# Expert gate and up projections as three fp32r products, with the rows stationary and the weights split a block ahead

## The chip, the cores and the metric

The kernel runs on one core of one Trainium2 chip. The metric is the time of one execution on the device in microseconds (us); 3158.83 us is the median of three executions of the kernel before. PE is the matrix engine, DVE the vector engine, ACT the scalar engine, POOL the GpSimd engine, SP the engine that here only issues transfers.

## The reference, cut to what matters

Two transformer blocks run on 1024 rows of 1024 floats. The first ends in a mixture of experts: each row goes to 2 of 32 experts. Rows are sorted by expert into blocks of 128, each block of one expert, and each block computes:

```python
def run_block(args):
    xb, e = args                                             # xb: 128 x 1024
    hid = jax.nn.silu(xb @ w_gate[e]) * (xb @ w_up[e])       # 1024 x 512 each
    return hid @ w_down[e]                                   # 512 x 1024

yb = lax.map(run_block, (buf.reshape(n_blocks, MOE_BLOCK, D), block_e)).reshape(n_rows, D)
y = jnp.zeros((T, D), jnp.float32).at[tok_s].add(yb[dest].astype(jnp.float32) * w_s[:, None])
```

All weights and rows are fp32. In the run profiled the routing makes 32 blocks. The rest of the two layers (a pooling and mLSTM mixer before, windowed, dilated and latent attention after) is not touched.

## The kernel before

`route` leaves, in SBUF, the row numbers of each block (`idx`), the expert of each block (`block_e`) and the number of blocks (`n_blocks`). `experts` then runs a loop over the blocks on every engine, with the block number in a register. Each engine has its own instruction order, written out by hand, and the engines meet at semaphores. `combine` then gathers the two rows of `y_dram` for each token.

A matmul's first operand is stationary (it is loaded into the array), its second moves. `D` is 1024 (`KT` = 8 slices of 128), the expert width 512 (`FT` = 4 slices), `GC` = 4 chunks of two slices. `HALF` is 512, one PSUM bank of fp32. In the profile a matmul's operands are printed moving first, then stationary.

For each block:

- SP loads gate and up in eight chunks of 512 KB, each into the place that PE has finished with (semaphore `used`), then the four chunks of down.
- POOL copies the block's row numbers to `idx` and gathers its 128 rows into `xg` with an indirect transfer.
- PE runs gate and up as plain fp32 products: the stationary operand is a 128 x 128 piece of the weights, the moving one is `xT`, the transposed rows. The result comes out transposed, as 4 slices of hid columns by 128 rows, so hid is already in the form that the down product needs. Then it transposes the next block's rows (`turn`, eight transposes), and runs down.
- Down is computed from fp32r parts. An fp32r operand is rounded to fewer bits. `high` is x rounded, `low` is x minus high, and a product of fp32 accuracy is high x high + high x low + low x high: `multiply_split`, three products.
- ACT makes the high parts of the down weights (L1309), DVE the low parts (`low_part`, L155). ACT computes Silu of gate; DVE multiplies by up and splits hid. Both copy `xT` from PSUM, and both copy half of the result to `y`; ACT issues the store.

The places of the gate and up weights are single: a chunk is loaded again while PE works on the others.

Of the kernel before, what the change touches and what calls it, by code (L numbers as in the profile page):

```python
# [8 lines left out]
ALU = mybir.AluOpType  # L9
ACT = mybir.ActivationFunctionType  # L10
AX = mybir.AxisListType
F32 = mybir.dt.float32
# [3 lines left out]
P = 128  # L16
S = 1024
# [1024 lines left out]
def route(nc, K, R, w_rg, b_rg, w_re, b_re, slot_tok):  # L1042
# [3 lines left out]
    with ExitStack() as ctx:  # L1046
# [27 lines left out]
        with nc.Block() as block:  # L1074
# [55 lines left out]
            def _(dve):  # L1130
# [69 lines left out]
                link(dve.tensor_copy(R["n_blocks"][:, :], pend[0:1, cur, EXPERTS - 1:EXPERTS]))  # L1200


def experts(nc, K, R, h_dram, y_dram, w_gate, w_up, w_down):
# [3 lines left out]
    CH = 2 * GC + FT  # L1207
    with ExitStack() as ctx:
        sc = Scope(nc, ctx, "moe")
        wg = sc.sb("wg", [P, KT, D_EXP])  # L1210
        wu = sc.sb("wu", [P, KT, D_EXP])
        wd = sc.sb("wd", [P, FT, D])
        xg = sc.sb("xg", [P, D])
        xT = sc.sb("xT", [P, KT, P])
        idx = sc.sb("idx", [P, 1], I32)
        sil = sc.sb("sil", [P, HALF])
        hid = sc.sb("hid", [P, FT, P])

        hid_parts = sc.sb("hid_parts", [P, 2, FT, P], F32R)
        wd_parts = sc.sb("wd_parts", [P, 2, FT, D], F32R)  # L1220
        wd_high, wd_split, hid_made = sc.sem("wd_high"), sc.sem("wd_split"), sc.sem("hid_made")
        y = sc.sb("y", [P, D])
        loaded = [sc.sem(f"w{c}") for c in range(CH)]
        used, gathered, idx_ready, xt_made, xt_act, xt_dve, sil_ready, hid_ready, y_act, y_dve, y_stored, settled, settled_act = [sc.sem(n) for n in
            ("used", "gathered", "idx_ready", "xt_made", "xt_act", "xt_dve", "sil_ready", "hid_ready", "y_act", "y_dve", "y_stored", "settled", "settled_act")]
        wg_d = w_gate.rearrange("e (c k p) f -> (e c) p k f", p=P, k=2)
        wu_d = w_up.rearrange("e (c k p) f -> (e c) p k f", p=P, k=2)
        wd_d = w_down.rearrange("e (c p) d -> (e c) p d", p=P)
        nb_ap = R["n_blocks"][0:1, 0:1]
        with nc.Block() as block:  # L1230
            @block.sync
            def _(sp):
                nb = sp.value_load(nb_ap, min_val=1, max_val=BLOCKS)
                with sp.Fori(0, nb) as i:
                    e = sp.value_load(R["block_e"][0:1, bass.ds(i, 1)], min_val=0, max_val=EXPERTS - 1)
                    for c in range(GC):

                        for which, (dst, src) in enumerate(((wg, wg_d), (wu, wu_d))):
                            n = 2 * c + which
                            sp.wait_ge(used, i * CH + n + 1)  # L1240
                            sp.dma_start(dst[:, 2 * c:2 * c + 2, :], src[bass.ds(e * GC + c, 1), :, :, :].rearrange("a p k f -> p (a k) f")).then_inc(loaded[n], 16)
                    for f in range(FT):
                        n = 2 * GC + f
                        sp.wait_ge(wd_split, i * FT + f + 1)
                        sp.dma_start(wd[:, f, :], wd_d[bass.ds(e * FT + f, 1), :, :].rearrange("a p d -> p (a d)")).then_inc(loaded[n], 16)

            @block.gpsimd
            def _(pool):
                nb = pool.value_load(nb_ap, min_val=1, max_val=BLOCKS)
                with pool.Fori(0, nb + 1) as i:  # L1250
                    pool.wait_ge(xt_made, i + 1)
                    pool.tensor_copy(idx[:, :], R["idx"][:, bass.ds(i, 1)]).then_inc(idx_ready, 1)
                    pool.wait_ge(idx_ready, i + 1)
                    pool.sem_inc(settled, 1)
                    pool.indirect_dma_start(out=xg[:, :], out_offset=None, in_=h_dram,
                                            in_offset=bass.IndirectOffsetOnAxis(ap=idx[:, 0:1], axis=0)).then_inc(gathered, 16)
                    pool.wait_ge(gathered, i * 16 + 16)

            def turn(pe):
                for k in range(KT):  # L1260
                    mm = pe.transpose(ps[:, 4 + k // 4, (k % 4) * P:(k % 4 + 1) * P], xg[:, k * P:(k + 1) * P], ident[:, :])
                mm.then_inc(xt_made, 1)

            @block.tensor
            def _(pe):
                pe.sem_inc(used, CH)
                pe.sem_inc(xt_made, 1)
                pe.wait_ge(gathered, 16)
                turn(pe)
                nb = pe.value_load(nb_ap, min_val=1, max_val=BLOCKS)  # L1270
                with pe.Fori(0, nb) as i:
                    pe.wait_ge(xt_act, i + 1)
                    pe.wait_ge(xt_dve, i + 1)
                    for c in range(GC):
                        for which, w in enumerate((wg, wu)):
                            pe.wait_ge(loaded[2 * c + which], i * 16 + 16)
                            for k in (2 * c, 2 * c + 1):
                                for f in range(FT):

                                    mm = pe.matmul(ps[:, which, f * P:(f + 1) * P], w[:, k, f * P:(f + 1) * P], xT[:, k, :],  # L1280
                                                   start=(k == 0 and f == 0), stop=(k == KT - 1), skip_group_check=True)
                            mm.then_inc(used, 1)
                    pe.wait_ge(gathered, i * 16 + 32)
                    turn(pe)
                    pe.wait_ge(y_act, i + 1)
                    pe.wait_ge(y_dve, i + 1)
                    for f in range(FT):
                        pe.wait_ge(wd_split, i * FT + (FT + f + 1))
                        if f % 2 == 0:
                            pe.wait_ge(hid_ready, i * 2 + (f // 2 + 1))  # L1290
                        for n in range(2):
                            cols = slice(n * HALF, (n + 1) * HALF)
                            mm = multiply_split(pe, ps[:, 2 + n, :], (hid_parts[:, 0, f, :], hid_parts[:, 1, f, :]),
                                                (wd_parts[:, 0, f, cols], wd_parts[:, 1, f, cols]), f == 0, f == FT - 1)
                        mm.then_inc(used, 1)

            @block.scalar
            def _(act):
                act.sem_inc(y_act, 1)

                act.dma_start(y_dram[BLOCKS * P:(BLOCKS + 1) * P, 0:P], ident[:, :]).then_inc(y_stored, 16)
                act.wait_ge(xt_made, 2)
                act.activation(xT[:, 0:4, :], ps[:, 4, :].rearrange("p (k t) -> p k t", t=P), ACT.Copy).then_inc(xt_act, 1)
                nb = act.value_load(nb_ap, min_val=1, max_val=BLOCKS)
                with act.Fori(0, nb) as i:
                    act.wait_ge(used, i * CH + CH)
                    for f in range(FT):
                        act.wait_ge(loaded[2 * GC + f], i * 16 + 16)
                        act.activation(wd_parts[:, 0, f, :], wd[:, f, :], ACT.Copy).then_inc(wd_high, 1)  # L1309
                    act.wait_ge(used, i * CH + (CH + 2 * GC - 1))  # L1310
                    act.activation(sil[:, :], ps[:, 0, :], ACT.Silu).then_inc(sil_ready, 1)
                    act.wait_ge(xt_made, i + 3)
                    act.activation(xT[:, 0:4, :], ps[:, 4, :].rearrange("p (k t) -> p k t", t=P), ACT.Copy).then_inc(xt_act, 1)
                    act.wait_ge(used, i * CH + 2 * CH)
                    act.wait_ge(y_stored, i * 16 + 16)
                    act.activation(y[:, 0:HALF], ps[:, 2, :], ACT.Copy).then_inc(y_act, 1)
                    act.wait_ge(y_act, i + 2)
                    act.wait_ge(y_dve, i + 2)
                    act.dma_start(y_dram[bass.ds(i * P, P), :], y[:, :]).then_inc(y_stored, 16)
                act.wait_ge(y_stored, nb * 16 + 16)  # L1320
# [3 lines left out]
            def _(dve):  # L1324
                dve.sem_inc(y_dve, 1)
                dve.sem_inc(wd_split, FT)
                dve.wait_ge(xt_made, 2)
                dve.tensor_copy(xT[:, 4:8, :], ps[:, 5, :].rearrange("p (k t) -> p k t", t=P)).then_inc(xt_dve, 1)  # L1328
                nb = dve.value_load(nb_ap, min_val=1, max_val=BLOCKS)
                with dve.Fori(0, nb) as i:  # L1330
                    for f in range(FT):
                        dve.wait_ge(wd_high, i * FT + (f + 1))
                        low_part(dve, wd_parts[:, 1, f, :], wd[:, f, :], wd_parts[:, 0, f, :]).then_inc(wd_split, 1)
                    dve.wait_ge(sil_ready, i + 1)
                    dve.wait_ge(used, i * CH + (CH + 2 * GC))
                    for q in range(2):
# [1856 lines left out]
```

## Time and profile before

| what | value |
|---|---|
| median of three executions | 3158.83 us (3152.17 to 3163.78) |
| the profiled execution | 3161.66 us |
| its span, first to last instruction | 3159.9 us |
| mean granted TensorE clock | 0.933 of full speed |
| PE busy | 2745.1 us, 87% |
| DVE busy | 1190.5 us, 38% |
| ACT busy | 989.1 us, 31% |
| POOL busy | 374.8 us, 12% |
| bytes moved | 451.17 MB, mean 143 GB/s |

Shares are of the whole span, over stages that have different limits. The expert stage takes about 700 us of it, from about 902 to 1605 us. Busy time of PE counts overlapping matmuls once. Times in the rows are microseconds from the start of the span unless they are marked ns.

### The profile page before, as it was taken

To read this page: it belongs to the slowest core of one execution; us is meant where nothing else is said; L and a number is where in the kernel's file an instruction comes from. 1 tells how busy PE (TensorE), PEld (TensorE's weight loads), DVE (VectorE), ACT (ScalarE), POOL (GpSimd) and SP (SyncE) were. 2 spreads that over 40 slices of the span, in tenths; PEclk is the share of its full clock that TensorE was granted. 3 is DMA by queue.
4 is the path that set the end of the run, shared out by engine and by line. 5 is a ranking of instruction groups with operands and counts; after the bars stand their busy time and mean duration, and the time that the engine had idled before them with its cause. 6 is when DMAs were issued, how large, how long until landed. Compare 5 with 4: busy or idle time off the path is not lost. (4 is left out here: it accounts for less than half of the span.)

```text
span 3159.9 us, 40572 instructions
## 1 busy us (share of the span) xinstructions
PE 2745.1 (87%) x15466; PEld 2277.5 (72%) x15466; DVE 1190.5 (38%) x2498; ACT 989.1 (31%) x1418; POOL 374.8 (12%) x388
## 2 busy tenths in 40 slices
PE   5999799989749999999928999788897988899996
PEld 3887666669749999999926888467797775455586
DVE  4542611122323433334343042366533124555522
ACT  4223311111013343344333153132323235344431
POOL 0000200000020000000021062223120000022120
PEclk9999899999569999999968999899999989999998
DMA  3110281120169999999954294466640312000121
GB/s 91 40 47 14 104 309 40 34 91 23 56 210 345 339 347 345 340 346 347 340 189 130 74 256 131 123 168 143 147 125 1 107 36 47 5 14 15 41 91 61
DMA packets 309981, 451.17 MB, mean 143 GB/s; under 512 B 89612, under 2 KB 183564, under 8 KB 309725
## 3 DMA queue, kind: packets, MB, share of 16 engines
q1 hardware_dynamic: 267664, 326.11, 32.6%
q0 software_dynamic: 26016, 89.15, 8.3%
q10 hardware_dynamic: 16172, 34.17, 3.2%
q8 instruction: 84, 1.38, 0.2%
q14 instruction: 45, 0.36, 0.0%
HBM read 354.88 MB, written 92.19 MB: 141 GB/s over the span
## 5 line engine op out<-in xcount | busy, mean ns | idle before, releaser
L1280 PE MATMUL ps<-moe_xT,moe_wg 128*128 128x128 f32 x2048 | 251.3, 276 | 1.0 <-DVE moe_xT L1328 1.0
L1280 PE MATMUL ps<-moe_xT,moe_wu 128*128 128x128 f32 x2048 | 250.2, 275 | 0.0
L1280 PEld LDWEIGHTS ps<-moe_xT,moe_wg 128*128 128x128 f32 x2048 | 242.9, 193 | 4.0 <-issue 1.4
L1280 PEld LDWEIGHTS ps<-moe_xT,moe_wu 128*128 128x128 f32 x2048 | 239.7, 192 | 0.0
L155 DVE TENSOR_TENSOR moe_wd_parts<-moe_wd,moe_wd_parts 128x1024 fp32r<-128x1024 f32 x128 | 148.5, 1220 | 113.4 <-ACT moe_wd_parts L1309 113.4
L2926 PE MATMUL ps<-lattn_pT,c_v 128*65 128x512 f32 (+3 forms) x384 | 150.6, 487 | 0.0
L2969 ACT ACTIVATE lattn_pT<-ps 128x512 f32<-128x512 f32 (+1 forms) x160 | 92.0, 575 | 186.8 <-PE ps L2912 185.6
L148 PE MATMUL ps<-ab_h,abp_w 128*128 128x512 f32 x336 | 134.1, 399 | 3.5 <-DVE abp_w L155 3.5
L149 PE MATMUL ps<-ab_h,abp_w 128*128 128x512 f32 x336 | 133.5, 397 | 0.0
L150 PE MATMUL ps<-ab_h,abp_w 128*128 128x512 f32 x336 | 133.4, 397 | 0.0
L316 PE MATMUL ps<-ident,n_h 128*128 128x128 f32 x256 | 38.6, 327 | 105.4 <-DVE n_h L290 62.5
L148 PE MATMUL ps<-mix_h,merge_w 128*128 128x512 f32 x256 | 115.2, 450 | 14.8 <-DVE merge_w L155 10.2
L1309 ACT ACTIVATE moe_wd_parts<-moe_wd 128x1024 fp32r<-128x1024 f32 x128 | 125.8, 1048 | 6.8 <-DMA moe_wd<-in_w_e_down_dram 6.4
L2164 PE MATMUL ps<-att_qx,att_kx 65*128 65x256 f32 (+1 forms) x512 | 111.7, 350 | 17.4 <-DVE att_sT L2359 17.4
L148 PE MATMUL ps<-moe_wd_parts,moe_hid_parts 128*128 128x512 f32 x256 | 103.1, 403 | 13.7 <-DVE moe_hid_parts L155 13.7
L316 PEld LDWEIGHTS ps<-ident,n_h 128*128 128x128 f32 x256 | 37.7, 174 | 106.2 <-DVE n_h L290 95.2
L3027 DVE TENSOR_REDUCE lattn_mxr<-ps 128x1 f32<-128x128 f32 (+6 forms) x112 | 77.3, 690 | 91.5 <-PE ps L2892 91.1
L2256 ACT ACTIVATE att_sT<-att_sT 128x512 f32<-128x512 f32 (+1 forms) x104 | 63.1, 613 | 147.8 <-DVE att_sT L2359 143.4
L2164 PEld LDWEIGHTS ps<-att_qx,att_kx 65*128 65x128 f32 x512 | 84.3, 199 | 26.4 <-issue 15.7
L149 PE MATMUL ps<-mix_h,merge_w 128*128 128x512 f32 x256 | 102.7, 401 | 0.0
L150 PE MATMUL ps<-mix_h,merge_w 128*128 128x512 f32 x256 | 102.7, 401 | 0.0
L148 PE MATMUL ps<-mix_h,proj_w 128*128 128x512 f32 x256 | 101.2, 396 | 0.0
(512 smaller groups left out, 6553.4 us busy)
## 6 DMA issues: line engine op xcount, KB each, us to landing
moe_wg<-in_w_e_gate_dram SPq DMA_DIRECT2D x128, 512.0 KB, 4.6
moe_wu<-in_w_e_up_dram SPq DMA_DIRECT2D x128, 512.0 KB, 4.8
moe_wd<-in_w_e_down_dram SPq DMA_DIRECT2D x128, 512.0 KB, 10.2
y_rows<-merge_zero POOLq DMA_DIRECT2D x49, 512.0 KB
y_rows<-moe_y ACTq DMA_DIRECT2D x32, 512.0 KB, 5.5
qk_parts<-abp_high POOLq DMA_DIRECT2D x58, 256.0 KB, 12.3
qk_parts<-abp_full POOLq DMA_DIRECT2D x58, 256.0 KB, 12.2
abp_raw<-in_ab_w_in_dram SPq DMA_DIRECT2D x22, 512.0 KB, 5.2
```

Source lines behind the costliest of these rows:

```text
L148: pe.matmul(out, a[0], b[0], start=start, stop=False)
L149: pe.matmul(out, a[0], b[1], start=False, stop=False)
L150: return pe.matmul(out, a[1], b[0], start=False, stop=stop)
L155: return dve.tensor_tensor(low, x, high.bitcast(F32), ALU.subtract)
L316: mm = pe.transpose(ps[:, u % 8, j * P:(j + 1) * P], h[:, half * 4 + j, k * P:(k + 1) * P], ident[:, :])
L1280: mm = pe.matmul(ps[:, which, f * P:(f + 1) * P], w[:, k, f * P:(f + 1) * P], xT[:, k, :], start=(k == 0 and f == 0), stop=(k == KT - 1), ...
L1309: act.activation(wd_parts[:, 0, f, :], wd[:, f, :], ACT.Copy).then_inc(wd_high, 1)
L2164: mm = pe.matmul(ps[:, 4 + g % 2, off:off + w], block_of(kx[0:HD + 1, s, :], c, r, n), queries, start=True, stop=True, skip_group_check=True)
L2256: act.activation(sT[:, g % SUMS, 0:total], sT[:, g % SUMS, 0:total], ACT.Exp, scale=SC_AB).then_inc(e_done, 1)
L2926: mm = pe.matmul(ps[0:C_V + 1, acc + half, q0 + skip - half * HALF:HALF], v, pT[:, g % SUMS, off + skip:off + n], start=(b == 0), stop=(j ...
L2969: act.activation(pT[:, g % SUMS, 0:total], ps[:, 4 + g % 2, 0:total], ACT.Exp, scale=C_SCALE).then_inc(e_done, 1)
L3027: dve.tensor_reduce(mxr[:, what:what + 1], src[:, 0:w], AX.X, ALU.max)
```

## The change

Gate and up become `multiply_split` products, as down is. Now the transposed rows are stationary (high and low part, `xT[:, 0]` and `xT[:, 1]`) and the weights move, 512 columns at a time. All three weights have a high, a low and a raw place: SP loads into the raw one, ACT writes high, DVE low; for two of the four down chunks POOL computes low (`ON_POOL`). The result of gate and up is now rows by columns, so hid is transposed by four further transposes (`turn_hidden`), and split from PSUM.

The loops are reordered: in iteration j PE runs gate of block j+1, the hid transposes of j, up of j+1, the row transposes of j+2 and down of j. ACT and DVE split gate and up of block j+2 in the same iteration. Block 0 and a part of block 1 stand ahead of the loop, the last two blocks' ends behind it; the loop runs `n_blocks - 2` times, and `n_blocks` becomes three numbers (n, n-1, n-2), with three more DVE operations in `route`.

The contraction index is laid out as `(p c k)` instead of `(c k p)`, so a partition of a chunk is one run of 4 KB of memory instead of two of 2 KB. To match, the row transposes read every eighth column of `xg` (`xg_cols`).

```diff
+        xT = sc.sb("xT", [P, 2, KT, P], F32R)
+        wg_d = w_gate.rearrange("e (p c k) f -> e p c (k f)", c=GC, k=2)
+        xg_cols = xg[:, :].rearrange("t (p k) -> t k p", k=KT)
+        ON_POOL = 2
...
             @block.sync
+                with sp.Fori(0, loops) as j:
+                    e = expert_of(j + 2)
+                    load_gate(j + 2, e)
+                    load_up(j + 2, e)
+                    load_down(j + 1, expert_of(j + 1))
...
             @block.gpsimd
+                def low_down(b):
+                    for i in range(ON_POOL):
+                        f = FT - ON_POOL + i
+                        pool.wait_ge(d_high, b * FT + (f + 1))
+                        pool.tensor_tensor(wd[1][:, f, :], wd[2][:, f, :], wd[0][:, f, :].bitcast(F32), ALU.subtract).then_inc(d_split_pool, 1)
+                with pool.Fori(0, loops) as j:
+                    low_down(j)
+                    gather(j + 3)
...
             @block.tensor
+                def gate_up(b, bank, w, split, used):
+                    for c in range(GC):
+                        pe.wait_ge(split, b * GC + (GC + c + 1))
+                        for k in range(2):
+                            n = 2 * c + k
+                            mm = multiply_split(pe, ps[:, bank, :], (xT[:, 0, n, :], xT[:, 1, n, :]), (w[0][:, c, k, :], w[1][:, c, k, :]), n == 0, n == KT - 1)
+                        mm.then_inc(used, 1)
+                with pe.Fori(0, loops) as j:
+                    gate(j + 1)
+                    turn_hidden(j)
+                    up(j + 1)
+                    turn_x(j + 2)
+                    down(j)
...
             @block.scalar
+                def high(b, w, loaded, used, n, made, c):
+                    act.wait_ge(loaded[c], b * 16 + 16)
+                    act.wait_ge(used, b * n + (c + 1))
+                    act.activation(w[0][:, c], w[2][:, c], ACT.Copy).then_inc(made, 1)
+                def out(b):
+                    act.wait_ge(d_used, b * FT + 2 * FT)
+                    act.wait_ge(y_stored, b * 16 + 16)
+                    act.activation(y[:, 0:HALF], ps[:, 2, :], ACT.Copy).then_inc(y_act, 1)
+                    act.wait_ge(y_act, b + 2)
+                    act.wait_ge(y_dve, b + 2)
+                    act.dma_start(y_dram[bass.ds(b * P, P), :], y[:, :]).then_inc(y_stored, 16)
+                with act.Fori(0, loops) as j:
+                    for f in range(FT - 1):
+                        high(j, wd, d_loaded, d_used, FT, d_high, f)
+                    silu(j + 1)
+                    hidden_high(j)
+                    high(j, wd, d_loaded, d_used, FT, d_high, FT - 1)
+                    for c in range(GC):
+                        high(j + 2, wg, g_loaded, g_used, GC, g_high, c)
+                    rows_high(j + 2)
+                    for c in range(GC):
+                        high(j + 2, wu, u_loaded, u_used, GC, u_high, c)
+                    out(j)
...
             @block.vector
+                with dve.Fori(0, loops) as j:
+                    for f in range(FT - ON_POOL):
+                        low(j, wd, FT, d_high, d_split, f)
+                    hidden_low(j)
+                    for c in range(GC):
+                        low(j + 2, wg, GC, g_high, g_split, c)
+                    hidden(j + 1)
+                    rows_low(j + 2)
+                    for c in range(GC):
+                        low(j + 2, wu, GC, u_high, u_split, c)
+                    out(j)
```

In SP's loop each gate and up chunk of block j+2 waits for the low part of the same chunk of block j+1, and each down chunk of j+1 for that of j. `silu`, `rows_high`, `hidden_high` on ACT and `rows_low`, `hidden`, `hidden_low` on DVE are one operation each on 512 PSUM columns, two for the rows. `hidden(j + 1)` waits for Silu and up of block j+1. `rows_high(j + 2)` waits for the row transposes of j+2 and for up of j+1, since `xT` is single. `down(j)` waits for `hidden_low(j)` and for the lows of each chunk.

## Rows read from the trace of the kernel before

**Rows 1.** The page's slices, 40 of 79 us each: granted clock, bytes.

```profile
PEclk9999899999569999999968999899999989999998
GB/s 91 40 47 14 104 309 40 34 91 23 56 210 345 339 347 345 340 346 347 340 189 130 74 256 131 123 168 143 147 125 1 107 36 47 5 14 15 41 91 61
```

**Rows 2.** Windows: length, busy us of PE, PEld, DVE, ACT, POOL, clock, DMA share, GB/s.

```profile
911.00:919.00 8.00, 6.81 (x31) 6.41 (x32) 0.69 (x1) 1.88 (x2) 1.17 (x2) 0.50 1.05 408
...
1100.00:1313.00 213.00, 208.73 (x1599) 196.66 (x1599) 81.17 (x120) 82.64 (x90) 13.82 (x20) 1.00 0.95 344
...
400.00:420.00 20.00, 17.51 (x62) 11.29 (x60) 1.27 (x2) 2.32 (x5) 0.17 (x1) 1.00 1.04 409
```

**Rows 3.** Timeline of one block: start, us, engine, line, what [idle before <-releaser].

```profile
1102.97 0.50 PE L148 MATMUL ps<-moe_wd_parts,moe_hid_parts 128*128 128x512 f32 x1 [0.43 <-DVE moe_hid_parts L155]
...
1108.31 0.40 PE L150 MATMUL ps<-moe_wd_parts,moe_hid_parts 128*128 128x512 f32 x1
...
1108.55 1.95 PE L1280 MATMUL ps<-moe_xT,moe_wg 128*128 128x128 f32 x16
...
1108.84 0.69 DVE L1348 COPY moe_y<-ps 128x512 f32<-128x512 f32 x1 [4.21 <-PE ps L150]
1109.76 0.34 ACTq L1319 DMA_DIRECT2D y_rows<-moe_y  x1
...
1110.54 1.28 ACT L1309 ACT_TABLE_LOAD   x1 [1.19 <-PE ps L1280]
...
1111.83 4.00 ACT L1309 ACTIVATE moe_wd_parts<-moe_wd 128x1024 fp32r<-128x1024 f32 x4
...
1112.92 4.63 DVE L155 TENSOR_TENSOR moe_wd_parts<-moe_wd,moe_wd_parts 128x1024 fp32r<-128x1024 f32 x4 [3.39 <-ACT moe_wd_parts L1309]
...
1115.85 1.28 ACT L1311 ACT_TABLE_LOAD   x1
...
1121.05 1.95 PE L1280 MATMUL ps<-moe_xT,moe_wu 128*128 128x128 f32 x16
1121.25 0.60 ACT L1311 ACTIVATE moe_sil<-ps 128x512 f32<-128x512 f32 x1 [4.12 <-PE ps L1280]
...
1122.84 1.04 PE L1261 MATMUL ps<-ident,moe_xg 128*128 128x128 f32 x8
...
1124.30 0.50 PE L148 MATMUL ps<-moe_wd_parts,moe_hid_parts 128*128 128x512 f32 x1 [0.43 <-DVE moe_hid_parts L155]
```

**Rows 4.** Timeline, the stage's first products and its last copy of y.

```profile
911.22 1.97 PE L1261 MATMUL ps<-ident,moe_xg 128*128 128x128 f32 x8 [45.06 <-DMA moe_xg<-h_rows,moe_idx]
...
914.16 3.78 PE L1280 MATMUL ps<-moe_xT,moe_wg 128*128 128x128 f32 x16 [0.98 <-DVE moe_xT L1328]
...
1599.40 0.60 ACT L1316 ACTIVATE moe_y<-ps 128x512 f32<-128x512 f32 x1 [5.57 <-PE ps L150]
```

**Rows 5.** Groups of instructions on DVE: count | busy us, mean ns | idle before.

```profile
L155 DVE TENSOR_TENSOR moe_wd_parts<-moe_wd,moe_wd_parts 128x1024 fp32r<-128x1024 f32 x128 | 148.5, 1220 | 113.4 <-ACT moe_wd_parts L1309 113.4
...
L155 DVE TENSOR_TENSOR lattn_kl<-ps,lattn_kh 64x512 fp32r<-64x512 f32 x32 | 21.9, 683 | 28.7 <-ACT lattn_kh L2951 28.7
```

**Rows 6.** Timeline of POOL and of DVE in a later stage.

```profile
2292.57 3.37 POOL L2102 TENSOR_TENSOR att_cp<-att_cp,att_rc 64x1024 f32<-64x1024 f32 x1 [15.71 <-DMA att_rc<-den_rows]
2296.02 2.39 POOL L2108 TENSOR_TENSOR ab_oT<-ab_oT,att_cp 64x1024 f32<-64x1024 f32 x1
...
2292.50 1.23 DVE L155 TENSOR_TENSOR att_out_low<-ab_oT,att_out_high 128x1024 fp32r<-128x1024 f32 x1 [1.65 <-ACT att_out_high L1692]
...
2296.57 2.93 DVE L155 TENSOR_TENSOR att_out_low<-ab_oT,att_out_high 128x1024 fp32r<-128x1024 f32 x1 [1.64 <-ACT att_out_high L1692]
```

**Rows 7.** The page's DMA issues: count, size, median us to landing.

```profile
moe_wd<-in_w_e_down_dram SPq DMA_DIRECT2D x128, 512.0 KB, 10.2
```

**Rows 8.** Timeline, last DVE operation of route and last scatter of POOL.

```profile
877.70 0.14 DVE L1200 CAST routed_n_blocks<-route_pend 1x1 int32<-1x1 f32 x1
...
893.02 0.97 POOL L1100 DMA_INDIRECT slot_tok<-route_tok,routed_dest  x1 [0.30 <-issue]
```

More of the change, by code:

```diff
@@ L1222, in experts @@
         y = sc.sb("y", [P, D])
[L1223 to L1227, printed above, removed]
@@ L1256, in _ @@
                                             in_offset=bass.IndirectOffsetOnAxis(ap=idx[:, 0:1], axis=0)).then_inc(gathered, 16)
[L1257 to L1262, printed above, removed]
+                    pool.wait_ge(gathered, b * 16 + 16)
+                def low_down(b):
[3 more added lines that the diff above has]
+                        pool.tensor_tensor(wd[1][:, f, :], wd[2][:, f, :], wd[0][:, f, :].bitcast(F32), ALU.subtract).then_inc(d_split_pool, 1)
@@ L1264, in _ @@
+                last, loops = blocks_less(pool, 1), blocks_less(pool, 2)
+                pool.sem_inc(d_split_pool, ON_POOL)
+                for b in range(3):
+                    gather(b)
+                with pool.Fori(0, loops) as j:
+                    low_down(j)
+                    gather(j + 3)
+                low_down(loops)
+                low_down(last)
             @block.tensor
             def _(pe):
-                pe.sem_inc(used, CH)
-                pe.sem_inc(xt_made, 1)
@@ L1268, in _ @@
[L1268 to L1273, printed above, removed]
-                    for c in range(GC):
[L1275 to L1286, printed above, removed]
-                    for f in range(FT):
-                        pe.wait_ge(wd_split, i * FT + (FT + f + 1))
-                        if f % 2 == 0:
-                            pe.wait_ge(hid_ready, i * 2 + (f // 2 + 1))
@@ L1291, in _, with down @@
+                def down(b):
+                    pe.wait_ge(h_low, b + 2)
+                    pe.wait_ge(y_act, b + 1)
+                    pe.wait_ge(y_dve, b + 1)
+                    for f in range(FT):
+                        if f < FT - ON_POOL:
+                            pe.wait_ge(d_split, b * (FT - ON_POOL) + (FT - ON_POOL + f + 1))
+                        else:
+                            pe.wait_ge(d_split_pool, b * ON_POOL + (f - FT + 2 * ON_POOL + 1))
                         for n in range(2):
@@ new lines, in down @@
+                        mm.then_inc(d_used, 1)
+                pe.sem_inc(g_used, GC)
+                pe.sem_inc(u_used, GC)
+                pe.sem_inc(d_used, FT)
+                pe.sem_inc(x_turned, 1)
+                pe.sem_inc(h_turned, 1)
+                last, loops = blocks_less(pe, 1), blocks_less(pe, 2)
+                turn_x(0)
+                gate(0)
+                up(0)
+                turn_x(1)
+                with pe.Fori(0, loops) as j:
[4 more added lines that the diff above has]
+                    down(j)
@@ L1297, in _, with silu @@
+                gate(last)
+                turn_hidden(loops)
+                up(last)
+                down(loops)
+                turn_hidden(last)
+                down(last)
             @block.scalar
             def _(act):
+                def high(b, w, loaded, used, n, made, c):
+                    act.wait_ge(loaded[c], b * 16 + 16)
+                    act.wait_ge(used, b * n + (c + 1))
+                    act.activation(w[0][:, c], w[2][:, c], ACT.Copy).then_inc(made, 1)
+                def silu(b):
+                    act.wait_ge(g_used, b * GC + 2 * GC)
+                    act.wait_ge(hid_ready, b + 1)
+                    act.activation(sil[:, :], ps[:, 0, :], ACT.Silu).then_inc(sil_ready, 1)
@@ new lines, in rows_high, with hidden_high @@
+                def rows_high(b):
+                    act.wait_ge(x_turned, b + 2)
+                    act.wait_ge(u_used, b * GC + GC)
+                    for n in range(2):
+                        act.activation(xT[:, 0, 4 * n:4 * n + 4, :], ps[:, 4 + n, :].rearrange("p (k t) -> p k t", t=P), ACT.Copy).then_inc(x_high, 1)
+                def hidden_high(b):
+                    act.wait_ge(h_turned, b + 2)
+                    act.wait_ge(d_used, b * FT + FT)
+                    act.activation(hT[:, 0, :, :], ps[:, 6, :].rearrange("p (f t) -> p f t", t=P), ACT.Copy).then_inc(h_high, 1)
@@ L1301, in _ @@
                 act.dma_start(y_dram[BLOCKS * P:(BLOCKS + 1) * P, 0:P], ident[:, :]).then_inc(y_stored, 16)
[L1302 to L1319, printed above, removed]
@@ L1321, in _ @@
+                for f in range(FT - 1):
+                    high(loops, wd, d_loaded, d_used, FT, d_high, f)
+                silu(last)
+                hidden_high(loops)
+                high(loops, wd, d_loaded, d_used, FT, d_high, FT - 1)
+                out(loops)
+                for f in range(FT):
+                    high(last, wd, d_loaded, d_used, FT, d_high, f)
+                hidden_high(last)
+                out(last)
+                act.wait_ge(y_stored, last * 16 + 32)
                 act.sem_inc(settled_act, 1)
@@ new lines, in low, with rows_low @@
+                def low(b, w, n, high, made, c):
+                    dve.wait_ge(high, b * n + (c + 1))
+                    low_part(dve, w[1][:, c], w[2][:, c], w[0][:, c]).then_inc(made, 1)
+                def rows_low(b):
+                    for n in range(2):
+                        dve.wait_ge(x_high, b * 2 + (n + 1))
+                        ks = slice(4 * n, 4 * n + 4)
+                        low_part(dve, xT[:, 1, ks, :], ps[:, 4 + n, :].rearrange("p (k t) -> p k t", t=P), xT[:, 0, ks, :]).then_inc(x_low, 1)
@@ new lines, in _ @@
+                last, loops = blocks_less(dve, 1), blocks_less(dve, 2)
+                rows_low(0)
+                for c in range(GC):
+                    low(0, wg, GC, g_high, g_split, c)
+                for c in range(GC):
+                    low(0, wu, GC, u_high, u_split, c)
+                for c in range(GC):
+                    low(1, wg, GC, g_high, g_split, c)
+                hidden(0)
+                rows_low(1)
+                for c in range(GC):
+                    low(1, wu, GC, u_high, u_split, c)
@@ L1351, in combine @@
+                for f in range(FT - ON_POOL):
+                    low(loops, wd, FT, d_high, d_split, f)
+                hidden_low(loops)
+                hidden(last)
+                out(loops)
+                for f in range(FT - ON_POOL):
+                    low(last, wd, FT, d_high, d_split, f)
+                hidden_low(last)
+                out(last)
 def combine(nc, K, R, y_dram):
```

153 lines of the change are left out of this document (98 added, 55 removed).

## The prediction

> **What bounds the kernel now.** I read the page first for the stage that the change touches. In the line of moved bytes the expert stage is the long plateau at about 345 GB/s, with the TensorE clock at its upper level of 2.4 GHz throughout [rows 1]. Both PE and the DMA engines look full there. The windows say which of them is [rows 2]: over ten blocks the DMA rate is 344 GB/s, but elsewhere in this trace the same engines hold 409 GB/s for 20 us. A block moves 6 MiB of weights, 0.5 MiB of gathered rows and 0.5 MiB of stored rows, 7.34 MB, so 344 GB/s is one block in 21.3 us and 409 GB/s would be one in 18.0 us. The transfers have 3.3 us of room; PE has none.
>
> The timeline of one block confirms it [rows 3]. From its first down matmul at 1102.97 to the next block's at 1124.30 are 21.33 us, all of it PE in turn: 24 down products until 1108.55 (5.58), eight groups of 16 gate and up products of 1.786 us each until 1122.84 (14.29), eight transposes and a short wait (1.46). ACT and DVE idle most of the time, and each of their operations is hidden by PE. That is what the change alters: it gives PE less and ACT and DVE much more.
>
> **The change, part by part.** *PE.* The 128 fp32 products (111.6 ns apart) become 48 fp32r products with 512 columns. Of these the 24 down products are the pattern: 5.58 us for 24 with their first wait, 5.5 without it. So gate and up take 11.0 instead of 14.29. Down stays at 5.5, the row transposes at 1.46, and four transposes of hid are new, half of the 1.04 for eight plus a small wait, 0.65. PE needs 18.6 us a block. The row transposes now read their stationary operand with a step of 8 floats, which no row here shows. Below I take nothing more; above, the 1.97 us of the first, slow turn [rows 4], so 0 to 0.9. Either is inside PE's slack below.
>
> *ACT.* 12 highs of 1024 columns instead of 4 (0.97 apart: four in 3.90 to 4.00), five operations from PSUM at 0.60 [rows 3], two table loads of 1.28, 0.78 from the store's issue to the loop's head: 18.1 us a block.
>
> *DVE.* 10 lows (four in 4.63: 1.22 for the last, 1.14 apart) and five operations on 512 PSUM columns at 0.69, 0.61 when they follow directly [rows 3, 5]: 14.8 us a block.
>
> *POOL.* Two lows a block. The nearest rows is its product of 64 x 1024 at 2.39 [rows 6]; I take 2.4, with 1.2 (DVE's time for such an operation) and 3.37 (the longest) as ends.
>
> *SP.* All three weights are loaded after the lows free the raw chunk, up to a block ahead. The latest against its use is wd, freed between 4.6 and 11.2 us after the ring's zero (below) and read a block later; 10.2 us to land [rows 7] fit. Cover: more than 10 us each. If it went, the highs would wait for DMA. Gather and store keep their size. The three added DVE operations on n_blocks (0.2 us each) run while POOL issues scatters for another 16 us, at nothing [rows 8].
>
> No engine's sum reaches 21.33, so read by sums alone this is a gain. But the sums of ACT and DVE are not run side by side: they wait for each other in order. ACT issues the store of y only when DVE has copied its half, and ACT's next instruction is the next iteration's first high, for which DVE waits. That closes a ring. Its zero is the end of DVE's copy of y (1109.53 in the block shown):
> - ACT issues the store, branches and loads its table at 1.0, its first high starts at 2.3, DVE's first low at 3.4. All three are differences in [rows 3]. DVE's two wd lows end at 5.75.
> - ACT's three highs end at 5.25, the Silu table load at 6.55, Silu at 7.15, the high of the transposed hid at 7.7. DVE takes its low, 7.75 to 8.4.
> - ACT's fourth wd high ends at 8.7, the first wg high at 9.65. DVE could start the four wg lows at 9.7.
> - POOL took its first low at 5.75 (DVE was in one until then), to 8.15, and the second from 8.8 to 11.2.
> - Four wg lows, hidden, two row lows, four wu lows, the copy of y.
>
> **POOL beside DVE.** At 2296.02 POOL starts a product of 2.39 us, and a DVE low that begins at 2296.57 lasts 2.93 instead of 1.23: it ends 1.09 after POOL's end. At 2292.57 it is POOL that starts second, and it lasts 3.37 instead of 2.4 [rows 6]. So a low that meets POOL's is held until POOL ends. Here DVE's first wg low would end at 12.3 instead of 10.9 and the fourth at 15.7 instead of 14.3. Then hidden ends at 16.3, the row lows at 17.5 (ACT made their highs by 13.8), the wu lows at 22.1 and the copy of y at 22.7. The ring takes 22.7 us with the hold, 21.3 without it. The reads from PSUM I leave unheld: 32 such lows have a mean of 683 ns [rows 5].
>
> The Trainium skill, page "SBUF — State Buffer", section "Who interferes with whom", has the rule for it: a DVE instruction with two SBUF inputs and a GpSimd instruction that reads SBUF exclude each other for a whole instruction, the first to start winning. By that rule the ring is 22.7, without it 21.3; the trace agrees with it.
>
> **Table loads.** In [rows 3] a load starts 0.02 after the activation before it and takes 1.28, and the next activation starts at once. So two loads cost 2.56 a block. The Trainium skill, page "ScalarE: Activation LUTs", section "What ACT_TABLE_LOAD costs", adds a drain of about 1.38 to each. By it the ring would be an estimated 25.5 us; the rows show no such drain, and the measurement decides.
>
> **Does PE keep up?** In ring time PE runs gate from -5.2 (the row lows end at 17.5 of the turn before) to 0.3, the hid transposes, up to 6.5, row transposes to 8, down from 8.5 (it needs the low of hid) to 14.1. ACT asks for gate at 6.55, for the row transposes at 12.6, DVE for down at 22.1. PE is ahead everywhere and idles 4.1 us a block.
>
> **Start and end.** Before, the first gate product is at 914.16 [rows 4] and the last block's copy of y on ACT at 1599.40: 685.2 us. Now DVE sets the first two blocks: eight lows from 915.5 end at 924.6, four wg lows of block 1 at 929.6, hidden and row lows at 931.4, four wu lows at 936.0. That is 3.4 in the ring, so its zero lies at 932.6, 18.4 after 914.16. After the 30 iterations, down of block 30 ends at 14.1, y at 15.1, then four highs (19), high and low of hid (20.3) and the last down (26): 26 us. In all 18.4 + 30 x 22.7 + 26 = 725.4, 40 us more than 685.2. The break-even ring is (685.2 - 18.4 - 26) / 30 = 21.36.
>
> **The sum.** The profiled execution took 3161.66 us, 2.8 over the median of the runs. 3161.7 + 40.2 = 3201.9, less 2.8: 3199 us.
>
> **The rivals.**
> - *No hold worth its name*, because POOL's low is short (1.2) or falls into a DVE gap. The ring is 21.3, the time 3157. For it: DVE idles 1.3 before the wg lows. Against: ACT makes the fourth wd high 0.95 before the first wg high, so POOL is just ahead.
> - *The ring doesn't close*, and PE sets the pace at 18.6, inside the DMA's 18.0: 30 x (18.6 - 21.36) = -83, 3076 us. This is the other side. It decides from a ring under 20.8, so 1.9 us of mine must be wrong. For it: ACT idles before the store, and 2.3 us of the ring's head (store, branch, table load) would vanish if it were not queued. Against: ACT is in order, and these 2.3 us stand in the rows.
> - *POOL is slower on 128 partitions*: at 3.37 each, the second ends at 12.5, the ring is 24.0, the time 3238.
> - *The clock falls.* PE idles 4.1 us a block. In the first 8 us after a long idle time it had the lower level of 1.2 GHz (0.50), and 16 products took 3.78 instead of 1.95 [rows 2, 4]. If it stayed there, PE alone would need some 36 us, 3158.8 + 30 x 14.6, about 3600 us. A few us of it each block are covered by the 8 us before DVE asks for down.
>
> **Chances.** Forecast 0.48 (own range 3180 to 3220: a ring of 22.1 to 23.4), no hold 0.20, PE sets the pace 0.12, slower POOL 0.15, clock 0.05. The range goes from just under the no-hold case to just over slower POOL, 3150 to 3240, and leaves 0.17 out. A measurement of this kernel tells 0.5% (16 us) from no change. Slower: forecast, slower POOL, clock and a little of no hold, 0.70. The same: the rest of no hold, 0.18. Faster: 0.12.
>
> **What would show it.** Right: the expert stage repeats every 22 to 23.4 us; ACT waits some 4 us for DVE's copy of y before its store; DVE waits for ACT at the head of the loop (3.4) and before the low of hid (2); one wg low in four lasts 2.5 instead of 1.22; PE idles some 4 us a block; DMA falls to about 323 GB/s. Wrong: PE without gaps and a period near 18.6, POOL's lows in DVE's gaps, a lower clock in the stage's windows, or highs that wait for DMA.

## The result and the profile after

The changed kernel takes 3135.61 us, median of eight executions (3124.24 to 3141.52), against 3152.18 us of before, also eight. The ratio is 0.9938, interval 0.9924 to 0.9953: 0.6% faster. The forecast of 3199 us, slower, was wrong in its sign and out of its range.

The line of moved bytes over the 40 slices of the page and the window over 200 us of the expert stage, which answer to [rows 1] and [rows 2]:

```profile
GB/s 92 39 47 16 87 329 41 34 86 29 57 199 371 355 354 362 361 352 359 287 174 134 78 277 106 141 163 147 151 110 20 88 36 47 5 15 15 42 92 61
```

```profile
1100.00:1300.00 200.00, 177.22 (x821) 143.62 (x820) 163.46 (x147) 136.64 (x168) 73.25 (x40) 1.00 0.96 355
```

PE is no longer full, DVE is busy for 163 of 200 us, and the clock in this window is at 2.4 GHz. The period is best read from DVE's copy of y, once a block. The timeline shows the copy of block 0 and of block 29, both as they stand in the trace:

```profile
951.56 0.68 DVE L1472 COPY moe_y<-ps 128x512 f32<-128x512 f32 x1
...
1548.50 0.68 DVE L1472 COPY moe_y<-ps 128x512 f32<-128x512 f32 x1
```

596.94 us over 29 blocks are 20.58 us each, where before it was 21.33 [rows 3]. I had forecast 22.7. From SP's first load to ACT's last copy of y the stage takes 676.7 us instead of 695.7: 19.0 us less. The rest of the difference between the two spans (25.8 us) stands ahead of the stage (4.4) and behind it (2.4), where nothing was changed.

One turn of the ring in the changed kernel, the timelines of DVE, ACT and POOL (start, us, what, [idle before <-releaser]):

```profile
1116.34 0.68 DVE L1472 COPY moe_y<-ps 128x512 f32<-128x512 f32 x1
1119.17 2.36 DVE L155 TENSOR_TENSOR moe_wd_low<-moe_wd_raw,moe_wd_high 128x1024 fp32r<-128x1024 f32 x2 [2.16 <-ACT moe_wd_high L1381]
1122.04 0.69 DVE L155 TENSOR_TENSOR moe_hT<-ps,moe_hT 128x512 fp32r<-128x512 f32 x1 [0.50 <-ACT moe_hT L1397]
1123.93 6.72 DVE L155 TENSOR_TENSOR moe_wg_low<-moe_wg_raw,moe_wg_high 128x1024 fp32r<-128x1024 f32 x4 [1.21 <-ACT moe_wg_high L1381]
...
1132.37 4.62 DVE L155 TENSOR_TENSOR moe_wu_low<-moe_wu_raw,moe_wu_high 128x1024 fp32r<-128x1024 f32 x4
1136.91 0.68 DVE L1472 COPY moe_y<-ps 128x512 f32<-128x512 f32 x1
...
1117.24 0.34 ACTq L1405 DMA_DIRECT2D y_rows<-moe_y  x1
1118.08 2.96 ACT L1381 ACTIVATE moe_wd_high<-moe_wd_raw 128x1024 fp32r<-128x1024 f32 x3 [6.38 <-issue]
1120.94 0.58 ACT L1386 ACTIVATE moe_sil<-ps 128x512 f32<-128x512 f32 x1
...
1131.38 0.60 ACT L1402 ACTIVATE moe_y<-ps 128x512 f32<-128x512 f32 x1
1137.82 0.34 ACTq L1405 DMA_DIRECT2D y_rows<-moe_y  x1
...
1121.12 5.05 POOL L1294 TENSOR_TENSOR moe_wd_low<-moe_wd_raw,moe_wd_high 128x1024 fp32r<-128x1024 f32 x2 [12.46 <-ACT moe_wd_high L1381]
```

The reader is to see three things. ACT has its half of y at 1131.98 and issues the store only at 1137.82, after DVE's copy: the ring is there. POOL's two lows fill 1121.12 to 1126.17, and the four gate lows that begin at 1123.93 take 6.72 us where the four up lows take 4.62: the hold is there. And between ACT's store and its first high, and between its highs and Silu, there is no table load. The groups of the whole stage have a single one, ahead of the loop:

```profile
L1386 ACT ACT_TABLE_LOAD x1 | 1.3, 1283 | 0.0
```

The kernel before had two of them on each of its 32 blocks:

```profile
L1309 ACT ACT_TABLE_LOAD x32 | 41.1, 1283 | 37.4 <-PE ps L1280 37.0 <-issue 0.4
L1311 ACT ACT_TABLE_LOAD x32 | 41.1, 1283 | 0.6
```

The waits from 1100 to 1300 us (who waited <- for whom, us in total, times, longest) say what PE lacks: the low of the rows, for which it waits 2.3 us a block.

```profile
DVE moe_wd_low L155 <- ACT moe_wd_high L1381: 19.5, 9, 2.2
DVE moe_wg_low L155 <- ACT moe_wg_high L1381: 12.0, 10, 1.2
...
PE ps L148 <- DVE moe_xT L155: 22.8, 10, 2.4
```

### The profile page after: what moved, and what is told of

Its sections match the earlier page's. It is cut to its first block and busy times, and to the rows that moved or that the text cites. A ratio compares the mean times of both kernels' runs of the same rounds, so it can differ in the third digit from the quotient of the medians.

```text
span 3134.1 us, 36862 instructions
## 1 busy us (share of the span) xinstructions
PE 2671.5 (85%) x13026; PEld 2130.6 (68%) x13026; DVE 1463.3 (47%) x2596; ACT 1171.6 (37%) x1674; POOL 565.5 (18%) x452
## 5 line engine op out<-in xcount | busy, mean ns | idle before, releaser
L1294 POOL TENSOR_TENSOR moe_wd_low<-moe_wd_raw,moe_wd_high 128x1024 fp32r<-128x1024 f32 x64 | 162.1, 2554 | 388.2 <-ACT moe_wd_high L1381 380.7
L155 DVE TENSOR_TENSOR moe_wg_low<-moe_wg_raw,moe_wg_high 128x1024 fp32r<-128x1024 f32 x128 | 211.8, 1712 | 37.9 <-ACT moe_wg_high L1381 37.7
L1381 ACT ACTIVATE moe_wd_high<-moe_wd_raw 128x1024 fp32r<-128x1024 f32 x128 | 128.4, 1052 | 196.6 <-issue 189.6
L148 PE MATMUL ps<-moe_wg_high,moe_xT 128*128 128x512 f32 x256 | 109.6, 428 | 63.8 <-DVE moe_xT L155 60.4
L155 DVE TENSOR_TENSOR moe_wu_low<-moe_wu_raw,moe_wu_high 128x1024 fp32r<-128x1024 f32 x128 | 147.7, 1210 | 0.1
L1381 ACT ACTIVATE moe_wu_high<-moe_wu_raw 128x1024 fp32r<-128x1024 f32 x128 | 124.9, 1064 | 0.0
L1381 ACT ACTIVATE moe_wg_high<-moe_wg_raw 128x1024 fp32r<-128x1024 f32 x128 | 124.6, 1052 | 0.0
L148 PE MATMUL ps<-mix_h,merge_w 128*128 128x512 f32 x256 | 114.4, 447 | 11.0 <-DVE merge_w L155 10.1
L148 PE MATMUL ps<-moe_wd_high,moe_hT 128*128 128x512 f32 x256 | 104.7, 409 | 6.4 <-DVE moe_hT L155 6.4
L149 PE MATMUL ps<-moe_wg_low,moe_xT 128*128 128x512 f32 x256 | 105.4, 412 | 0.0
```

The source lines that it names most:

```text
L148: pe.matmul(out, a[0], b[0], start=start, stop=False)
L149: pe.matmul(out, a[0], b[1], start=False, stop=False)
L155: return dve.tensor_tensor(low, x, high.bitcast(F32), ALU.subtract)
L1294: pool.tensor_tensor(wd[1][:, f, :], wd[2][:, f, :], wd[0][:, f, :].bitcast(F32), ALU.subtract).then_inc(d_split_pool, 1)
L1381: act.activation(w[0][:, c], w[2][:, c], ACT.Copy).then_inc(made, 1)
```

## The experiments

All ratios are to the kernel before the change, timed on the same chip. Two theories stand against each other. By the ring theory DVE and ACT in turn set the period, and only what lies on that ring counts. By the DMA theory the transfers set it: the window of the changed kernel shows them busy for 0.96 of the time at 355 GB/s. PE itself is not a candidate there, since it waits 2.3 us a block for DVE.

**The table loads put back.** The change runs the first block's Silu ahead of the loop, so the loop is entered with the table it also ends with. One Exp behind that undoes it:

```diff
...
+                act.activation(other[:, :], K["ones"][:, 0:1], ACT.Exp)
                 with act.Fori(0, loops) as j:
```

> The changed kernel with one Exp of a single column on ACT ahead of its loop, so that the loop is entered with another activation table than it ends with; the two table loads per iteration that the kernel before had should stand in the loop again. Ring theory (ACT and DVE in turn set the period, 20.58 us in the changed kernel): each load of 1.28 us lies on the ring, 2.56 us in all, of which POOL's hold on DVE gives back some 0.6; period 22.3 to 23.1 us, 30 times, 52 to 77 us over the changed kernel, near what was predicted (3199 us). DMA theory (the transfers, 355 GB/s at a share of 0.96, set the period): ACT has some 5 us of waiting a block, the loads are hidden there, no change.

3199.94 us, ratio 1.014 (1.0105 to 1.0174): slower than before the change, and within a microsecond of what I had forecast for the change itself. That the two agree so closely is in part luck: the kernel before had a median of 3155.21 us in that session, so the loss was 45 us where I had forecast 40. ACT's and DVE's timelines of one turn, and the window:

```profile
1115.81 1.28 ACT L1382 ACT_TABLE_LOAD   x1 [5.93 <-issue]
1117.10 2.96 ACT L1382 ACTIVATE moe_wd_high<-moe_wd_raw 128x1024 fp32r<-128x1024 f32 x3
1120.08 1.28 ACT L1387 ACT_TABLE_LOAD   x1
1121.37 0.60 ACT L1387 ACTIVATE moe_sil<-ps 128x512 f32<-128x512 f32 x1
...
1114.07 0.68 DVE L1474 COPY moe_y<-ps 128x512 f32<-128x512 f32 x1
1118.20 2.36 DVE L155 TENSOR_TENSOR moe_wd_low<-moe_wd_raw,moe_wd_high 128x1024 fp32r<-128x1024 f32 x2 [3.44 <-ACT moe_wd_high L1382]
1122.49 0.69 DVE L155 TENSOR_TENSOR moe_hT<-ps,moe_hT 128x512 fp32r<-128x512 f32 x1 [1.94 <-ACT moe_hT L1398]
1124.38 6.00 DVE L155 TENSOR_TENSOR moe_wg_low<-moe_wg_raw,moe_wg_high 128x1024 fp32r<-128x1024 f32 x4 [1.20 <-ACT moe_wg_high L1382]
...
1136.64 0.68 DVE L1474 COPY moe_y<-ps 128x512 f32<-128x512 f32 x1
...
1100.00:1300.00 200.00, 171.71 (x750) 137.93 (x749) 142.77 (x135) 146.19 (x168) 63.88 (x36) 0.95 0.92 325
```

The period is 1136.64 - 1114.07 = 22.57 us, 1.99 more. DVE's waits say how it adds up: 3.44 instead of 2.16 at the head, 1.94 instead of 0.50 before the low of hid, and a hold that is 0.72 shorter: 1.28 + 1.44 - 0.72 = 2.00. The DMA theory falls here: the rate drops from 355 to 325 GB/s, and a cost on ACT alone moves the time. The granted clock is a little lower in this window, 0.95, but that isn't the cause: DVE's copies of y come every 22.6 us where the clock is 1.00 (1120 to 1140 us) as where it is 0.85 (1200 to 1220 us).

**Silu ahead of the loop of the kernel before.** The same from the other side:

```diff
...
                 nb = act.value_load(nb_ap, min_val=1, max_val=BLOCKS)
+                act.activation(other[:, :], K["ones"][:, 0:1], ACT.Silu)
                 with act.Fori(0, nb) as i:
```

> The kernel before the change with one Silu of a single column on ACT ahead of its loop. Theory that the loads stand in a loop because it is entered with another table than the one it ends with: both loads of each of the 32 iterations go from the trace, one is left ahead of the loop. Theory that they belong to the loop's head and to Silu: 64 loads stay. The time: PE sets the period there at 21.33 us and ACT waits, so no change either way, within 0.2%.

The groups of its stage have one load left of the 64 of before, and the time is the same: ratio 1.0002 (0.9986 to 1.0018).

```profile
L1306 ACT ACT_TABLE_LOAD x1 | 1.3, 1283 | 0.2 <-issue 0.2
```

So the loads follow from the table that stands at the loop's entry, not from Silu or the loop's head. The time says nothing about the ring, since ACT waits in this kernel; it was expected not to move.

**POOL without its lows.**

```diff
-                        pool.tensor_tensor(wd[1][:, f, :], wd[2][:, f, :], wd[0][:, f, :].bitcast(F32), ALU.subtract).then_inc(d_split_pool, 1)
+                        pool.sem_inc(d_split_pool, 1)
...
-                            mm = multiply_split(pe, ps[:, 2 + n, :], (hT[:, 0, f, :], hT[:, 1, f, :]), (wd[0][:, f, cols], wd[1][:, f, cols]), f == 0, f == FT - 1)
+                            mm = multiply_split(pe, ps[:, 2 + n, :], (hT[:, 0, f, :], hT[:, 1, f, :]), (wd[0][:, f, cols], wd[1 if f < FT - ON_POOL else 0][:, f, cols]), f == 0, f == FT - 1)
```

> The changed kernel with POOL's two subtractions a block left out (the low part of half of the down weights isn't made; the down product takes the high part in its place, so PE does as many products). Ring theory with the hold: the four gate lows fall from 6.72 to 4.63 us, the period from 20.58 to 18.5 to 18.8 us; 54 to 62 us less than the changed kernel, 3075 to 3082 us. Ring without the hold: no change, 3136 us. Theory that DMA sets the period: no change.

3080.46 us, ratio 0.9763 (0.9743 to 0.9783). DVE's timeline:

```profile
1107.02 4.63 DVE L155 TENSOR_TENSOR moe_wg_low<-moe_wg_raw,moe_wg_high 128x1024 fp32r<-128x1024 f32 x4 [1.20 <-ACT moe_wg_high L1381]
...
1125.50 4.63 DVE L155 TENSOR_TENSOR moe_wg_low<-moe_wg_raw,moe_wg_high 128x1024 fp32r<-128x1024 f32 x4 [1.20 <-ACT moe_wg_high L1381]
```

The four gate lows take 4.63 instead of 6.72, 2.09 less, and the period falls from 20.58 to 18.48, by 2.1. DVE's own waits (1.20 here) are as before. The hold is worth its whole length. The DMA theory fails again: the rate rises to 396 GB/s in the window from 1100 to 1300 us.

**All down lows on DVE.** This computes everything:

```diff
-        ON_POOL = 2
+        ON_POOL = 0
...
-                    for f in range(FT - ON_POOL):
+                    for f in range(FT - 1):
                         low(j, wd, FT, d_high, d_split, f)
                     hidden_low(j)
+                    low(j, wd, FT, d_high, d_split, FT - 1)
...
```

> The changed kernel with all four down lows on DVE, none on POOL; the fourth stands behind the low of hid. DVE gets 2.3 us more work a block, the hold of 2.1 us goes, and the two waits of DVE for ACT (0.5 and 1.2 us) are filled by the added work. Ring theory: the period is about 19.0 us, 45 us less in all, about 3090 us. Theory that DVE's busy time counts and not the order: 0.2 us longer a block, 6 us more. DMA theory: no change.

3091.99 us, ratio 0.9791 (0.9762 to 0.982). DVE's copies of y are at 1100.70 and 1119.57:

```profile
1100.70 0.69 DVE L1471 COPY moe_y<-ps 128x512 f32<-128x512 f32 x1
1103.55 3.50 DVE L155 TENSOR_TENSOR moe_wd_low<-moe_wd_raw,moe_wd_high 128x1024 fp32r<-128x1024 f32 x3 [2.16 <-ACT moe_wd_high L1380]
1106.97 0.68 DVE L155 TENSOR_TENSOR moe_hT<-ps,moe_hT 128x512 fp32r<-128x512 f32 x1
1107.57 1.22 DVE L155 TENSOR_TENSOR moe_wd_low<-moe_wd_raw,moe_wd_high 128x1024 fp32r<-128x1024 f32 x1
1108.70 4.63 DVE L155 TENSOR_TENSOR moe_wg_low<-moe_wg_raw,moe_wg_high 128x1024 fp32r<-128x1024 f32 x4
...
1119.57 0.69 DVE L1471 COPY moe_y<-ps 128x512 f32<-128x512 f32 x1
```

The period is 18.87. DVE has two lows more and is 1.71 us a block faster: only the wait at the head of the loop (2.16) is left of its idle time. The engine that was to be relieved by POOL was faster without that help.

**The store of y on POOL.** ACT no longer waits for DVE before its next highs:

```diff
+                def store(b):
+                    pool.wait_ge(y_act, b + 2)
+                    pool.wait_ge(y_dve, b + 2)
+                    pool.dma_start(y_dram[bass.ds(b * P, P), :], y[:, :]).then_inc(y_stored, 16)
...
                 with pool.Fori(0, loops) as j:
                     low_down(j)
                     gather(j + 3)
+                    store(j)
...
-                    act.wait_ge(y_act, b + 2)
-                    act.wait_ge(y_dve, b + 2)
-                    act.dma_start(y_dram[bass.ds(b * P, P), :], y[:, :]).then_inc(y_stored, 16)
...
```

> The changed kernel with the store of y issued by POOL behind its gather instead of by ACT, so that ACT doesn't wait for DVE's half of y before its next highs: the ring is cut open. Ring theory: DVE's wait at the head of the loop (2.15 us) goes, as do most of its waits inside, and PE sets the period at 18.3 to 18.6 us; about 60 us less, 3076 us. DMA theory: the period stays at 20.6 us or falls only to what 409 GB/s allow (18.0) with PE waiting for weights.

3084.48 us, ratio 0.9776 (0.9745 to 0.9808). DVE's timeline again:

```profile
1116.40 0.68 DVE L1477 COPY moe_y<-ps 128x512 f32<-128x512 f32 x1
1117.00 2.34 DVE L155 TENSOR_TENSOR moe_wd_low<-moe_wd_raw,moe_wd_high 128x1024 fp32r<-128x1024 f32 x2
1119.27 0.68 DVE L155 TENSOR_TENSOR moe_hT<-ps,moe_hT 128x512 fp32r<-128x512 f32 x1
1121.01 7.31 DVE L155 TENSOR_TENSOR moe_wg_low<-moe_wg_raw,moe_wg_high 128x1024 fp32r<-128x1024 f32 x4 [1.07 <-ACT moe_wg_high L1390]
...
1134.58 0.68 DVE L1477 COPY moe_y<-ps 128x512 f32<-128x512 f32 x1
```

The period is 18.18. The wait at the head is gone. The hold is longer (the four lows take 7.31) and costs little now, but not nothing. PE is busy for 198.77 of the 200 us from 1100 to 1300, yet it still starts a block's gate products only when DVE has the low of the rows: that ends at 1130.12, and the first product starts at 1130.35, 0.44 us after the last down product, where it is 0.24 us in the next version.

**Both.** All lows on DVE and the store on POOL.

> All down lows on DVE and the store of y on POOL, both changes together. With the ring cut open the period was 18.18 us, and PE had no idle time left; DVE with 17.0 us of work a block is under that. PE or DMA as the bound: as with the store on POOL alone, 18.1 to 18.2 us, 3080 to 3086 us. Hold still of weight, though the ring is open: up to 0.5 us less a block, 3070 us. DVE as the bound: longer than 18.2 us.

3073.38 us, ratio 0.9748 (0.973 to 0.9767). The interval overlaps that of the store on POOL alone, so the times don't tell the two apart; the periods in their traces do. ACT copies y at 1112.34 and 1130.24, a period of 17.90. The window shows PE without a gap:

```profile
1100.00:1300.00 200.00, 200.00 (x941) 165.51 (x940) 186.86 (x190) 158.66 (x192) 28.03 (x33) 1.00 1.02 410
```

The period is 0.28 us shorter than with the store on POOL alone, of the 0.5 that I had allowed the hold. The version differs from that one only in where the down lows are made, and 0.20 us of the 0.28 are the shorter gap ahead of the gate products.

**Rows of 2 KB.** The layout of the weights of the kernel before in this version:

```diff
-        wg_d = w_gate.rearrange("e (p c k) f -> e p c (k f)", c=GC, k=2)
+        wg_d = w_gate.rearrange("e (c k p) f -> (e c) p k f", p=P, k=2)
...
-        xg_cols = xg[:, :].rearrange("t (p k) -> t k p", k=KT)
+        xg_cols = xg[:, :].rearrange("t (k p) -> t k p", k=KT)
...
```

> Both changes, and gate and up weights laid out as in the kernel before: each partition's part of a chunk is two runs of 2 KB instead of one of 4 KB, and the row transposes read their stationary operand without a step. If DMA has no reserve at a period of 18.2 us and 2 KB runs carry at most the 396 GB/s that the kernel before reached in its first blocks: 18.5 us a block, 10 us longer than with 4 KB runs. If PE is the bound: no change, or a little less if the stepped transposes cost PE time (at most 0.2 us a block, 6 us).

3067.9 us, ratio 0.9719 (0.9695 to 0.9743), a period of 17.88 us and 413 GB/s. The interval overlaps that of the version with 4 KB runs; the 10 us that I had expected against it did not come. My ceiling of 396 GB/s was wrong.

**Fewer products.** One product of each gate and up slice left out:

```diff
-                            mm = multiply_split(pe, ps[:, bank, :], (xT[:, 0, n, :], xT[:, 1, n, :]), (w[0][:, c, k, :], w[1][:, c, k, :]), n == 0, n == KT - 1)
+                            pe.matmul(ps[:, bank, :], xT[:, 0, n, :], w[0][:, c, k, :], start=n == 0, stop=False)
+                            mm = pe.matmul(ps[:, bank, :], xT[:, 1, n, :], w[1][:, c, k, :], start=False, stop=n == KT - 1)
```

> Both changes, with one of the three products of each gate and up slice left out (high rows by low weights are not computed, and the last product takes the low weights), so that PE has 16 products less, 3.6 us a block. PE as the bound at 18.2: the period falls to what the next engine allows, DVE 17.0 us; 36 us less. DMA as the bound, 7.34 MB at 409 GB/s or 18.0 us: at most 5 us less in all.

3048.76 us, ratio 0.9669 (0.9649 to 0.9689): 25 us under the version with all products, between the 5 and the 36 of the two theories. The period explains 13 of them (0.43 us on each of 30 turns) and the start and the end of the stage 5 more, as the stage takes 583.7 us in this trace and 601.9 in that of the version with all products; where the rest comes from I don't know. ACT's copies of y come every 17.5 us, and now ACT waits for weights:

```profile
ACT moe_wg_high L1390 <- DMA moe_wg_raw<-in_w_e_gate_dram: 18.6, 24, 0.9
ACT moe_wd_high L1390 <- DMA moe_wd_raw<-in_w_e_down_dram: 15.3, 32, 1.0
```

```profile
1100.00:1300.00 200.00, 174.43 (x771) 138.98 (x770) 191.92 (x195) 165.67 (x196) 51.13 (x34) 0.96 1.03 420
```

PE was the bound at 17.9, since less work on it shortens the period. The next one is most likely DMA, at 420 GB/s or 17.5 us: six slices of the page in a row read 420, and ACT's highs wait for their weights. DVE, busy for 191.92 of the 200 us, is close behind, and no run tells the two apart.

**Both, with the table loads.** The Exp of the first experiment in the fast version:

> Both changes (all lows on DVE, the store on POOL; period 17.90 us) with the Exp ahead of the loop, so that the two table loads stand in it again. Theory that the loads cost by lying on the ring: with the ring open they only add to ACT's own work, 15.5 + 2.6 = 18.1 us a block, so the period goes to 18.1 to 18.5 us, 6 to 18 us in all. Theory that a load costs its time wherever it stands: 2.0 to 2.6 us a block as in the changed kernel, 60 to 77 us.

3069.04 us, ratio 0.9728 (0.9707 to 0.9748), a period of 17.90 us: no change. ACT's timeline shows both loads:

```profile
1112.81 0.60 ACT L1411 ACTIVATE moe_y<-ps 128x512 f32<-128x512 f32 x1 [0.49 <-PE ps L150]
1113.43 1.28 ACT L1390 ACT_TABLE_LOAD   x1
...
1118.34 1.28 ACT L1395 ACT_TABLE_LOAD   x1 [0.66 <-PE ps L150]
...
1130.71 0.60 ACT L1411 ACTIVATE moe_y<-ps 128x512 f32<-128x512 f32 x1 [0.49 <-PE ps L150]
```

They fit into what ACT had been waiting. Without them it waited 2.11 us before Silu, 0.93 before the rows and 0.73 before its copy of y; with them 0.66, nothing and 0.49, 2.62 less in all. The same two instructions that cost 2.0 us a block on the ring cost nothing beside it. My 18.1 was too high: ACT is busy for 186.49 of the 200 us, loads included, which is 16.7 us a block.

## Why the prediction was wrong

**The step that failed** is "Table loads": "So two loads cost 2.56 a block". The price is right, the number of loads was not. I carried the two loads of [rows 3] into the new loop because the new loop has the same mixture of Copy and Silu. But the change also runs one Silu ahead of the loop, and with that the loop needs none. Two experiments show it from both sides, one in each kernel. With the loads put back the ring took 22.57 us, against my 22.7: the rest of it was right. Without the loads, and with nothing else altered, my ring is 22.7 - 2.56 = 20.1 us; measured were 20.58, because the hold grows by 0.72 when the loads go.

**Point by point:**
- *PE a block, 18.6*: 17.9 (the version without a gap). *PE keeps up*: yes, it waits 2.3 us a block for the low of the rows; I had said 4.1 with the longer ring.
- *Price of a load, 1.28*: right, and the next activation starts 0.01 us after it (1115.81 + 1.28 against 1117.10). No drain is seen in this kernel either; with one the ring would have been 25.5 us, not 22.57.
- *The ring*: right. DVE's wait at the head was forecast as 3.4 and is 3.44 with the loads, 2.16 without. The two other waits for ACT, forecast as 2.0 and 1.3, are 1.94 and 1.20 with the loads. The experiment with the loads in place took 3199.94 us, and its period was 22.57.
- *The hold*: right in kind, a little small in size. I had four gate lows in 6.0 us; they took 6.00 with the loads and 6.72 without, as POOL's two lows of 2.5 us then follow each other without a gap. Of the rivals, "no hold worth its name" is refuted: it costs 2.1 us a block. The reads from PSUM are unheld, as I had taken them: the low of hid at 1122.04 takes 0.69 in the middle of POOL's two lows.
- *ACT's wait for DVE's copy of y, 4*: 5.6 (1131.98 to 1137.59).
- *Start and end*, 44.4 us together: 20.58 x 30 + 44.4 - 685.2 is -23.4, the stage gave -19.0. So they are 4 us longer than I had worked out.
- *DMA hidden*: yes. A block's bytes take at most 17.5 us, since the transfers reached 420 GB/s; I had 18.0 at 409.
- *Clock*: nearly as forecast. It is 1.00 from 1100 to 1300 us but 0.97 from 1300 to 1500. At 1401.7, 1.5 us after PE had waited 2.42 us for the low of the rows, it falls to its lower level for 3.4 us, and the gate products come 0.43 us apart instead of 0.23. The copies of y at 1383.88, 1404.46 and 1425.04 keep their 20.58: PE has that much slack, which is how I had expected a few us to be covered.

The term accounts for the miss: the ring is 2.1 us shorter than forecast, 1.99 of it by the loads as measured and the rest because my 22.7 was a little long. That is 64 us over 30 iterations, start and end give 4 back, together 60, and the forecast for the stage was 59 us above what was measured (+40.2 against -19.0).

The range was wrong for the same reason. "The ring doesn't close" was my rival for faster, and I had even counted the head's table load among what would have to vanish. But I gave it a chance as a whole (0.12) and asked why ACT would not be in order, not whether the load would be there.

## What to carry to other kernels

When two engines wait for each other once an iteration, follow one turn of that ring and add it up; sums of busy time said 18.6 us here, while the ring said 22.7 with two table loads (measured 22.57) and 20.1 without (measured 20.58). Instructions that only the compiler puts in, such as activation table loads, aren't carried over from the old loop to a new one: ask which table the loop is entered with and which it leaves. And before moving work to POOL to relieve DVE, look at what DVE does meanwhile: here the kernel was faster with all of the lows on DVE (ratio 0.979 against 0.994), and cutting the ring at its store as well brought 0.975.

## What the runs showed of the hardware

- DMA moved 420 GB/s over 200 us in the version with fewer products, 413 with runs of 2 KB and 410 with runs of 4 KB, more than the 409 of [rows 2] and the 396 of before's first blocks. A busy share of 0.96 did not mean that the period was set by DMA: at 355 GB/s it still had some 15% to give, as the 410 show. The Trainium skill, page "HBM Reference", section "Specifications (TRN2)", gives a core some 358 GB/s as its share and about 425 when it streams alone, bounded by its DMA engines. This kernel has one core; these three windows (410, 413 and 420) lie between the two figures, and the highest is near the second.
- A stationary operand read with a step of 8 floats loads in 193 ns instead of 141 (median of 256 each, version with 4 KB and with 2 KB runs), and it doesn't show in the period: 17.90 and 17.88. The two versions differ in the length of the DMA runs too.
- A DVE low with both inputs in SBUF takes 1.21 us by itself (the median) and up to 3.41 beside POOL's lows. It goes both ways: POOL's two lows took 5.05 us in the changed kernel and 6.35 with the store on POOL, where they begin in the middle of DVE's own (spans on POOL are rough).
